# A two-block kernel at its expert stages: the router's weights ahead in POOL's queue, the gathering in high and low parts, the last pieces of weights in halves

## What is computed

```python
def routed_moe(h2d, router_w, router_b, w_gate, w_up, w_down):      # layers 0 and 1
    aff = jax.nn.sigmoid(jnp.dot(h2d, router_w).astype(F32))
    sel = (aff + router_b.astype(F32)).reshape(n_tok, N_GROUPS, EXPERTS_PER_GROUP)
    ...                                                             # best group, its two best experts
    hid = jax.nn.silu(xblk @ w_gate[e]) * (xblk @ w_up[e])
    return hid @ w_down[e]

def expert_choice_ffn(h, w_router, w_e_gate, w_e_up, w_e_down):     # the second block
    cap = EC_FACTOR * length // N_EXPERTS
    aff = jax.nn.softmax((h @ w_router).astype(jnp.float32), axis=-1)
    top_aff, top_idx = lax.top_k(jnp.swapaxes(aff, 1, 2), cap)
    xe = jax.vmap(lambda hb, ib: hb[ib])(h, top_idx)
    hid = jax.nn.silu(jnp.einsum('becd,edf->becf', xe, w_e_gate)) * jnp.einsum('becd,edf->becf', xe, w_e_up)
    ye = jnp.einsum('becf,efd->becd', hid, w_e_down) * top_aff[..., None].astype(h.dtype)
    return jax.vmap(lambda ib, yb: jnp.zeros((length, d), yb.dtype).at[ib.reshape(-1)].add(yb.reshape(-1, d)))(top_idx, ye)
```

## Time and profile before

| | |
|---|---|
| median of 3 runs | 2904.63 us (2903.8 to 2908.11) |
| the profiled execution's own time | 2903.06 us |
| its span | 2901.6 us |
| TensorE, matmul | 2351.7 us busy (81%) |
| TensorE, weight load | 1442.4 us (50%) |
| VectorE | 1257.5 us (43%) |
| ScalarE | 975.1 us (34%) |
| POOL | 109.4 us (4%) |
| read from memory | 781.56 MB, written 37.90 MB |
| mean granted TensorE clock | 0.927 of full |

### The profile page before, as it was taken

One profiled execution on the slowest core, in us unless ns is written; L12 is line 12 of the kernel. 1 busy time (PEld: TensorE's weight loads), 2 busy tenths in 40 slices (PEclk: granted clock), 3 DMA queues, 4 the chain that ended last, 5 costly groups with the idle time before them and its releaser, 6 DMA issues.

```text
span 2901.6 us, 30543 instructions
## 1 busy us (share of the span) xinstructions
PE 2351.7 (81%) x12425; PEld 1442.4 (50%) x12425; DVE 1257.5 (43%) x1964; ACT 975.1 (34%) x1538; POOL 109.4 (4%) x179
## 2 busy tenths in 40 slices
PE   5977878499999998798497777759989978767776
PEld 3744656388888886543232222228667652222222
DVE  2487456489999996453200000034575350000001
ACT  3354323278887885242100000034444340000000
POOL 1010300100000000100100000000000000000000
PEclk8988988799999998898699999979999989999998
DMA  9288910299999995683799999963103439999997
GB/s 351 91 295 301 334 57 30 108 342 390 392 392 395 392 384 185 246 289 121 284 396 401 402 402 401 406 229 116 58 18 133 160 126 367 409 409 409 409 409 284
DMA packets 247398, 821.56 MB, mean 283 GB/s; under 512 B 11107, under 2 KB 11273, under 8 KB 246992
## 3 DMA queue, kind: packets, MB, share of 16 engines
q1 hardware_dynamic: 226688, 753.88, 67.6%
q0 software_dynamic: 14432, 45.54, 4.6%
q10 hardware_dynamic: 6128, 20.07, 1.8%
HBM read 781.56 MB, written 37.90 MB: 282 GB/s over the span
## 4 chain that ended last, share of the span: by engine, by line
PE 57%; DMA 26%; DVE 9%; ACT 3%; issue 2%; SPq 1%; POOL 1%; DVEq 0%; PEldq 0%; ACTq 0%; POOLq 0%
PE PS L255 54%; DMA ring<-in_moe_w_up 8%; DMA ring<-in_w_e_up 6%; DMA ring<-in_moe_w_gate 4%; DMA ring<-in_w_e_down 3%; DMA ring<-in_w_e_gate 2%; PE PS L1869 1%; DVE hgrn L1021 1%; DMA ring<-in_moe_w_down 1%; DMA ring<-in_ada_w 1%; SPq L392 1%; DVE SM L2505 0%; PE PS L568 0%; DVE cut L428 0%; DVE hgrn L1011 0%
## 5 line engine op out<-in xcount | busy, mean ns | idle before, releaser
L428 DVE TENSOR_TENSOR cut<-ring,cut 128x1024 fp32r<-128x1024 f32 x492 | 584.4, 1222 | 251.2 <-ACT cut L420 239.7
L420 ACT CAST cut<-ring 128x1024 fp32r<-128x1024 f32 x492 | 508.8, 1053 | 344.8 <-PE PS L255 316.9
L255 PE MATMUL PS<-cut,xeT 128*128 128x512 f32 x1536 | 365.9, 395 | 3.3 <-DVE cut L428 3.2
L255 PEld LDWEIGHTS PS<-cut,xeT 128*128 128x128 f32 x1536 | 286.7, 189 | 68.2 <-DVE cut L428 6.4
L255 PE MATMUL PS<-ring,hidT 128*64 128x512 f32 (+1 forms) x1024 | 237.7, 614 | 76.4 <-DMA ring<-in_w_e_down 38.5
L255 PE MATMUL PS<-ring,xeT 128*64 128x512 f32 x1024 | 236.9, 609 | 69.0 <-DMA ring<-in_moe_w_up 34.3
L255 PE MATMUL PS<-ring,XE 128*32 128x512 f32 x1008 | 228.6, 608 | 66.1 <-DMA ring<-in_w_e_up 41.3
L255 PE MATMUL PS<-cut,parts 128*128 128x512 f32 x864 | 212.2, 408 | 27.8 <-DVE cut L428 18.1
L255 PE MATMUL PS<-parts,cut 128*128 128x512 f32 x864 | 204.8, 397 | 3.6 <-DVE cut L428 3.6
L255 PEld LDWEIGHTS PS<-cut,parts 128*128 128x128 f32 x864 | 169.2, 197 | 72.1 <-issue 18.7
L255 PEld LDWEIGHTS PS<-ring,xeT 128*64 128x64 f32 x1024 | 75.8, 139 | 228.7 <-issue 168.8
(11 more groups left out here) (545 smaller groups left out, 2456.7 us busy)
## 6 DMA issues: line engine op xcount, KB each, us to landing
ring<-in_moe_w_gate SPq DMA_DIRECT2D x64, 2048.0 KB, 12.8
ring<-in_moe_w_up SPq DMA_DIRECT2D x64, 2048.0 KB, 12.6
ring<-in_moe_w_down SPq DMA_DIRECT2D x64, 2048.0 KB, 12.4
ring<-in_w_e_up SPq DMA_DIRECT2D x32, 2048.0 KB, 23.5
ring<-in_w_e_down SPq DMA_DIRECT2D x32, 2048.0 KB, 23.6
ring<-in_w_e_gate SPq DMA_DIRECT2D x31, 2048.0 KB, 23.6
ring<-in_ada_w SPq DMA_DIRECT2D x24, 2048.0 KB, 11.4
ring<-in_w_in SPq DMA_DIRECT2D x13, 2048.0 KB, 7.7
```

Of the source, the lines that this page charges most:

```text
L255: return pe.matmul(o, l, r, start=start, stop=stop, **kw)
L420: act.copy(self.bufs[i % len(self.bufs)][0], w).then_inc(self.high.sem, 1)
L428: dve.tensor_tensor(low, w, high.bitcast(F32), ALU.subtract).then_inc(self.low.sem, 1)
```

## The change

**Weights of the last stage.** The first three pieces get the ring's buffers of the mixing's last three pieces and are issued ahead of the meeting, each as its predecessor is cut up; the five free buffers come after the meeting. The last two pieces are issued as four halves by turns, and TensorE waits for the second halves in the middle of the pair.

**Router stages.** The six loads of `second_inputs_gpsimd` go behind the router's weights and bias in layer 1. The sums of the logits stand behind `nch // 2` groups of transposes in both layers: 2 for layer 0, 1 for layer 1.

**Gathering.** ScalarE writes the rows as `HH` in the rounded format, VectorE makes the rest `HL` (four subtractions), `SS` is of the rounded format, and each bank gets four products of one pass in place of two in float32: high parts of four banks first, then low parts. `SW` is made behind the subtractions, in other room, and no longer waited for by the gathering. The four banks that hold the rows are written last.

**End.** The sums are announced by half row, ScalarE squares halves as they come, and VectorE adds the two halves' squares.

```diff
-    W.place((3, 4, 8, 11, 9), moe2, end2, once=(9,), going=moe2 - 3)
+    W.place((), moe2, end2, extra=(3, 4, 8, 11, 9), once=(9,), first=moe2 + 3, going=moe2 - 3)
...
             pool.dma_start(rb, to_all(I["router_b"], 16)).then_inc(rb_in.sem, 16)
+            if layer:
+                second_inputs_gpsimd()
...
-                if t == 4:
+                if t == nch // 2:
                     route_sums()
...
-            if nch == 2:
-                route_sums()
...
     def second_inputs_gpsimd():
-        after_meeting(pool, met[pe].n)
...
-    second_inputs_gpsimd()
     wide_ring_sync()
...
     def choice_sync():
+        sync_pieces(moe2, moe2 + 3)
         after_meeting(sp, after_mix)
-        sync_pieces(moe2, end2)
+        sync_pieces(moe2 + 3, end2 - 2)
+
+        for half in range(2):
+            for n in (end2 - 2, end2 - 1):
+                if half == 0:
+                    sp.wait_ge(*consumed(W.prev[n]))
+                dst, _ = piece(next_key[n])
+                sl = slice(2 * half, 2 * half + 2)
+                sp.dma_start(dst[:, sl, :], W.rows[n][0][:, sl, :]).then_inc(last_halves.sem if half else landed(n)[0], 16)
...
-        for k in range(8):
+
+        def rows_of(part, k, first, last_):
             for c in xc:
-                last = mm(bank(k), H[:, c, k * P:(k + 1) * P], SS[:, c, :, :].rearrange("p e s -> p (e s)"), c == 0, c == 1)
-            last.then_inc(xe_made.sem, 1)
+                ins = mm(bank(k), part(c)[:, k * P:(k + 1) * P], SS[:, c, :, :].rearrange("p e s -> p (e s)"),
+                         first and c == 0, last_ and c == 1)
+            return ins
+
+        for k in XE_BANKS[:4]:
+            rows_of(lambda c: HH[:, c, :], k, True, False)
+        pe.wait_ge(*row_low(3))
+        for i, k in enumerate(XE_BANKS):
+            if i > 3:
+                rows_of(lambda c: HH[:, c, :], k, True, False)
+            rows_of(lambda c: HL[c], k, False, True).then_inc(xe_made.sem, 1)
...
+        for t in range(4):
+            c, g = divmod(t, 2)
+            sl = slice(512 * g, 512 * g + 512)
+            dve.wait_ge(*row_made(t))
+            dve.tensor_tensor(HL[c][:, sl], bank(ROW_BANKS[t]), HH[:, c, sl].bitcast(F32), ALU.subtract).then_inc(row_low.sem, 1)
...
+                    if i == 2 and both[1][1] == end2 - 1:
+                        pe.wait_ge(*last_halves(1))
...
-        for c in xc:
-            if c:
-                act.wait_ge(*f_squared(0))
-            act.activation(hid[0], bank(2 * c, 2), ACT.Square, accum_out=rs[:, c:c + 1]).then_inc(f_squared.sem, 1)
+        for h in range(2):
+            for c in xc:
+                k = 2 * h + c
+                act.wait_ge(*summed(k))
+                act.activation(hid[c][:, h * 512:h * 512 + 512], bank(2 * c + h), ACT.Square,
+                               accum_out=rs[:, k:k + 1]).then_inc(f_squared.sem, 1)
```

More of the change, by code:

```diff
@@ L3440, in program @@
     norm3 = normed(xc, 6, 8, H, HT2, XS, None)
+    last_halves = S.new("last_halves", "sp_q", 16)
     def choice_gpsimd():
@@ L3497, in choice_scalar @@
             act.wait_ge(*row_turned(t))
[L3498 to L3500 removed]
+            act.copy(HH[:, c, 512 * g:512 * g + 512], bank(ROW_BANKS[t])).then_inc(row_made.sem, 1)
+        for i in (1, 3, 5, 7):
+            k = XE_BANKS[i]
+            act.wait_ge(*xe_made(i))
             act.copy(XE[:, k, :], bank(k)).then_inc(odd_taken.sem, 1)
@@ L3609, in experts_tensor @@
                     last = mm(bank(2 * c + h), SWT[:, g, c * P:(c + 1) * P], YE[:, g, h * 512:h * 512 + 512], g == 0, g == 3)
-        last.then_inc(summed.sem, 1)
+                    if g == 3:
+                        last.then_inc(summed.sem, 1)
     def experts_scalar():
```

46 lines of the change are left out of this document (25 added, 21 removed).

## The result

The changed kernel takes **2886.59 us** (median of 4 runs, 2884.88 to 2888.16) against 2904.22 (4 runs, 2901.90 to 2908.11): a ratio of 0.9938, 95% interval 0.9921 to 0.9955, 17.6 us less. In a second comparison it came to 2886.38 us (6 runs) against 2902.64 (11 runs), 0.9940 (0.9928 to 0.9951). The forecast was 2884.6, 2878 to 2892.

What follows compares the result with a forecast made beforehand. Full-rate weight transfers were taken to bound the last two expert stages, so earlier restarts shorten the end. Gains 0.8 + 7.5 + 7.8 + 3.2 = 19.3 us off 2903.06, plus 0.8 towards the median: 2884.6 us, range 2878 to 2892.

Steps and rivals of the forecast that it cites:

- The step on which all rests: Last two expert stages: each microsecond TensorE starts sooner on the first piece is one at the end, if the stock has landed.
- Layer 0's sums: Layer 0's router: sums of the logits start behind eight transposes instead of sixteen, gaining 0.8 us.
- Layer 1: Layer 1's router stage: earlier load 8.1 plus earlier sums 1.7 less scatter loss 2.3, gaining 7.5 us (4 to 11).
- I take 2.3: Layer 1's scatter beside the last stock weights: a loss between 0 and 3 us, taken as 2.3.
- Three pieces ahead: Last stage: three weight pieces issued before the meeting into idle engines, by itself worth nothing.
- the cover for the next part: Last stage: early pieces let the stock land by 2401, so TensorE's 8 us earlier start isn't held up by arriving pieces.
- The gathering: Last stage: 32 one-pass products in 10.1 us, begun 1.35 us sooner, ending 7.8 us sooner (3.7 to 9.3).
- The end: Program's end: last pair as halves 2.2 us, squares by half rows 1.0, together 3.2 us (1.7 to 4.5).
- the load isn't faster by its place: Layer 1's router load: weights beside it, not its queue place, delay it; time 2886.9 us; chance 12%.
- the restart isn't moved: One of two expert stages keeps its restart, stock late or scatter slower; a 7.6 us term lost, 2892; chance 8%.
- The clock stays low: Through the gathering and first pairs, one-pass products being too little work; price 4.1 us, 2888.7; chance 10%.
- Slower: Last stage's changed buffer order lowers the weight rate; at 385 GB/s the kernel ends 8 us later; chance 3%.

Runs made afterwards that it cites:

- four edits: Each alone on the changed kernel: gate spread behind first pairs (2881.84 us), first two refills halved (2882.43), full-precision gathering and whole squares restored (2893.79), all eight pieces behind meeting (2887.54).
- the ninth piece held: Changed kernel, with SP issuing the ninth and last piece of layer 1's stock only once the gathered rows are in; 2882.05 us.
- the loads put back: Changed kernel, with POOL's six second-input loads (ctx first) ahead of the router's weights in layer 1 again; 2888.25 us.
- three edits: Changed kernel with layer 1's last stock piece held for the gathered rows, last-stage gate spread behind two pairs, and its first two refills halved; 2876.92 us.
- no three ahead: Changed kernel, with all eight pieces of the last stage's stock issued behind the meeting again; 2887.54 us.
- gathering back: Changed kernel, with the gathering as 16 full-precision products and the final squares as two of 1024 again; 2893.79 us.
- three edits with none ahead: The kernel with all three edits, but no piece of the last stage issued ahead of the meeting; 2879.41 us.
- first refills as halves: Changed kernel, with the last stage's first two refills sent as halves, the first halves after half of TensorE's first pair; 2882.43 us.

## Why the prediction was right, and where not

The step on which all rests, a microsecond sooner at the first piece is one at the end, held in the last stage up to the last pair but one: four edits moved the refill by -3.6, -3.4, +4.8 and 0.0 us, and that pair by -3.5, -3.4, +4.8 and 0.1. At the ring's end they moved it by -3.5, -3.4, +3.1 and -1.5: which pairs meet the low clock adds or takes 1.7 us there, and the prediction had nothing on it. Between m1 and m2 it held less exactly. Against before, m2 is 6.3 us sooner for 6.0 at the refill; with the ninth piece held, 6.9, 6.9 and 3.5 sooner for 5.8, 5.8 and 4.0; and with the loads put back the refill was 3.9 us later than in the changed kernel and m2 0.4 sooner.

- *Layer 0's sums*: 0.6 us were seen at the rows of layer 0 (0.8 forecast; undone, the logits are 1.0 later), but m1 is at 1379.67 us against 1379.65. The stretch between repeats to about a microsecond only (850.1 to 851.4 us from layer 0's meeting to m1), so whether the end has any of it can't be told.
- *Layer 1*: 7.5 forecast. Load and sums gave 10.6 us at the logits against the sum's 9.8 (8.1 + 1.7); the 0.9 left for the range, the shorter product (1.07 us for 1.93), came. The term that failed is "I take 2.3", and its bound of 3: the scatter lost 4.8 us. Four parts make the 2.5 between: 2.3 was taken where the sum gave 2.7; the scatter was issued 0.6 us sooner than reckoned, which its end, set by the bytes of both, doesn't give back; the last bytes went at 1414.5 and not at 1413.4, as more weights were due (2.5 MB behind 1402.7, by their packets in the trace, where 2.3 were reckoned) and the engines ran empty one after another; and this end of the bytes was set against a landing, which came at 1414.9. The time from the last byte to the landing was 0.4 us here and 0.3 in the kernel before, so it explains little. From 1407 to 1409 the two queues shared the engines about evenly, the weights with 109 packets and the scatter with 101; but the scatter's first packet came only at 1406.4, 4.3 us behind its issue, where without weights beside it, in the kernel before, it came 1.6 us behind. As the engines were full meanwhile (a share of 1.03, 410 GB/s), that doesn't move the end of the bytes. Net at the refill: 6.0 us.
- *Three pieces ahead*: "worth nothing" by itself is right, "the cover for the next part" is wrong: undone, the stage is the same within 0.2 us up to the last pair but one. By the prediction's own numbers the eight pieces were in at 2416 (2375 and 41), and the first buffer free at 2416.0 (2416.66 less 7.8, and 7.1 for the pair): a tie, called a cover. With a refill at 34.9 us behind the entry they are worth 4.7 us at the last pair but one, and 1.8 at the ring's end.
- *The gathering*: the first product is 8.9 us sooner against the entry, 7.8 forecast: the clock rose 3.5 us after TensorE's beginning and not 5.6, and the 32 products took 9.0 us and not 10.1. What the sum didn't have is the pair behind: at a clock of 0.50 for 3.4 us it took 1.7 us more (8.78 and not 7.1). "What comes behind (turning, copy, meeting) is unchanged, and the restart moves by the same" is the sentence that failed. Net at the refill 7.2 us: that this is near 7.8 is two errors against each other.
- *The end*: halves 1.55 (2.2, the middle of 1.4 and 3.1), squares 1.4 (1.0). Both ends of the first were seen. With the clock at a mean of 0.81 in the last pair but one the two take 15.6 us (16.8 with the three edits, at 0.83 over both); in three of the other kernels (no three ahead, gathering back, three edits with none ahead) they took 13.93, 3.2 us less than the 17.17 of the whole pieces. Which of the two a kernel gets was not forecast; the middle of both was near by luck.
- *Sum*: from the positions, 0.0 us up to m1, 6.3 from there to m2 (995.0 us before, 988.6 after), 7.2 to the refill, 0.2 in the stream, 1.6 in the last two pairs and 1.3 behind the ring: 16.6. The forecast had 0.8, 7.5, 7.8 and 3.2 for the end. So 0.8, 1.2 and 0.6 us are missing, and 0.1 at the end; the largest single mis-sized term is the scatter, 2.5 us, partly made up for at the logits (0.8) and behind the rows. The total is nearer than its parts.
- *Rivals*: "the load isn't faster by its place" and "the restart isn't moved" fell. "The clock stays low" came true in a small form (0.50 for 3.4 us, not through). "Slower" by the order of the buffers fell: from 2450 to 2830 us both kernels moved 409 GB/s.

## What to carry to other kernels

Where a stage is one long stream of weights with a full stock ahead of it, look at the idle stretch of the transfers: what counts is when the first buffer is given back, so put nothing between the meeting and the first piece that can wait, and refill from half a piece. Let nothing of the stock be in flight beside a transfer that the start waits for (here the last scatter landed 8.88 us behind its issue with the weights beside it, and 4.16 with one piece held); the last piece of it, held until that transfer was through, went into the idle stretch. Price work in front of a stage together with the clock that the first products behind it get (here 0.50 for 3.4 us, a price of 1.7), and read a gain at the last landing and at the last product: here they differed by up to 3 us.

## What was not expected of the hardware

- TensorE's granted clock fell from 1.00 to 0.50 for 3.4 us although it was busy 3.20 of the 4 us ahead (2398 to 2402). The engine had done transposes and four products with 12 rows; with the products moved away it stayed at 1.00.
- Five small loads of 30 KB or less ahead of a 64 KB one on its queue cost it 2.2 us of transfer (8.88 for 6.73) and 3.1 of issuing; 1 MB ahead of them cost 2.8 more (11.71).
- The transfer engines were busy alike at unlike rates in the last stage: a share of 0.99 with 360 GB/s (three edits, 2400 to 2416), 1.02 with 404 (first refills as halves, 2408 to 2424) and with 408 (no three ahead, 2404 to 2416).
- A scatter to memory issued while SP's weights kept the transfer engines full (410 GB/s) had its first packet only 4.3 us behind its issue, in place of 1.6; behind that the two queues shared the engines about evenly (109 and 101 packets from 1407 to 1409 us).
